# Routed experts' rows: places in one large table, or sums in two token tables

## The reference, cut to what matters

```python
def moe_ffn(x, router_w, router_bias, w1, w3, w2, sw1, sw3, sw2):
    ...
    _, idx = lax.top_k(scores + router_bias.astype(F32), TOP_K)      # TOP_K = 8 of 64
    gates = gates / jnp.sum(gates, -1, keepdims=True) * ROUTED_SCALE
    ...
        y = (jax.nn.silu(h @ w1[e]) * (h @ w3[e])) @ w2[e]           # h: the rows routed to e
        return y.astype(F32) * gate[:, None]
    ...
    routed = jnp.zeros((T, D), F32).at[row_tok].add(ys.reshape(n_rows, D))
    shared = (jax.nn.silu(xf @ sw1) * (xf @ sw3)) @ sw2
    return (routed + shared.astype(F32)).astype(x.dtype).reshape(B, S, D)
...
        x = layer_norm(DN_ALPHA * x + ffn, ln2_g[l], ln2_b[l])
```

## Time and profile before

| | |
|---|---|
| median of 3 runs | 2184.23 us (2182.27 to 2187.38) |
| profiled execution, its own time | 2186.5 us |
| its span, first to last instruction | 2184.7 us |
| PE busy | 2080.8 us, 95% |
| DVE busy | 1642.6 us, 75% |
| ACT busy | 1409.2 us, 65% |
| POOL busy | 581.3 us, 27% |
| moved by DMA | 572.78 MB |
| mean granted clock of PE | 0.978 |

### The profile page before, as it was taken

The page is one execution under the profiler, slowest core; times in us unless marked ns, Lnnn a source line. Parts: engine busy times, 40 slices in busy tenths (PEclk is TensorE's granted clock), DMA queues, the critical chain, the costliest instruction groups (busy, mean ns, idle before and its releaser), DMA issues. The chain is left out here.

```text
span 2184.7 us, 32260 instructions
## 1 busy us (share of the span) xinstructions
PE 2080.8 (95%) x10998; PEld 1689.3 (77%) x10998; DVE 1642.6 (75%) x2419; ACT 1409.2 (65%) x1778; POOL 581.3 (27%) x336
## 2 busy tenths in 40 slices
PE   6999989899999999999888999898999999999996
PEld 4778878688888888887376888777888888888862
DVE  2486453699999999998345944537999999999955
ACT  3443762488888888887045347426888888888841
POOL 0010200133443444442011021002344434434310
PEclk9999999999999999999999999999999999999998
DMA  6312213599999999995741140265999999999938
GB/s 202 97 30 72 113 67 147 196 378 377 389 378 379 375 387 386 382 382 223 302 145 59 51 162 1 76 252 192 382 378 393 378 375 382 376 382 380 379 128 359
DMA packets 136052, 572.78 MB, mean 262 GB/s; under 512 B 32356, under 2 KB 58468, under 8 KB 82712
## 3 DMA queue, kind: packets, MB, share of 16 engines
q1 hardware_dynamic: 99096, 504.37, 60.5%
q0 software_dynamic: 36864, 67.19, 8.0%
HBM read 560.41 MB, written 78.14 MB: 292 GB/s over the span
## 5 line engine op out<-in xcount | busy, mean ns | idle before, releaser
L1430 POOL DMA_INDIRECT rows<-x_rows,index x122 | 281.4, 2307 | 129.8 <-issue 69.5
L1587 DVE TENSOR_TENSOR w_next_lo<-w_next,w_hi 128x2048 fp32r<-128x2048 f32 x128 | 292.8, 2288 | 0.1
L1587 DVE TENSOR_TENSOR w_lo<-w,w_hi 128x2048 fp32r<-128x2048 f32 x124 | 285.2, 2300 | 2.0 <-ACT w_hi L1635 1.4
L1635 ACT CAST w_hi<-w 128x2048 fp32r<-128x2048 f32 x124 | 236.4, 1906 | 51.0 <-PE ps_sum L1493 51.0
L1635 ACT CAST w_hi<-w_next 128x2048 fp32r<-128x2048 f32 x128 | 243.5, 1902 | 35.4 <-PE ps_sum L1493 35.4
L1491 PE MATMUL ps_sum<-w_hi,rowsT_first_hi 128*128 128x512 f32 x512 | 208.8, 408 | 9.1 <-PEq L151 9.1
L1491 PE MATMUL ps_sum<-w_hi,rowsT_hi 128*128 128x512 f32 x512 | 208.0, 406 | 4.4 <-DVE rowsT_lo L1599 4.4
L1516 PE MATMUL ps_sum<-w_hi,hiddenT_hi 128*128 128x512 f32 x512 | 201.8, 394 | 3.9 <-DVE hiddenT_lo L1606 3.9
L1493 PE MATMUL ps_sum<-w_hi,rowsT_first_lo 128*128 128x512 f32 x512 | 202.9, 396 | 0.0
L1493 PE MATMUL ps_sum<-w_hi,rowsT_lo 128*128 128x512 f32 x512 | 202.3, 395 | 0.0
L1518 PE MATMUL ps_sum<-w_hi,hiddenT_lo 128*128 128x512 f32 x512 | 201.8, 394 | 0.0
(11 more groups left out here) (286 smaller groups left out, 5283.3 us busy)
## 6 DMA issues: line engine op xcount, KB each, us to landing
w_next<-exp_w SPq DMA_DIRECT2D x192, 1024.0 KB, 10.1
w<-exp_w SPq DMA_DIRECT2D x128, 1024.0 KB, 9.6
w_first<-exp_w SPq DMA_DIRECT2D x32, 1024.0 KB
w_last<-exp_w SPq DMA_DIRECT2D x32, 1024.0 KB
wbuf<-w_in SPq DMA_DIRECT2D x16, 1024.0 KB, 5.5
got<-y_rows SPq DMA_DIRECT2D x8, 2048.0 KB, 21.3
got<-y_rows SPq DMA_DIRECT2D x16, 1024.0 KB, 24.3
w_out_sb<-w_out SPq DMA_DIRECT2D x2, 4096.0 KB, 19.3
```

Of the source, the lines that this page charges most:

```text
L1430: pool.indirect_dma_start(rows[0:CAP, x.slot, :], None, d["x1_rows"], bass.IndirectOffsetOnAxis(ap=index[0:CAP, x.step, 0:1], axis=0), bou ...
L1587: dve.tensor_tensor(w13_lo[x.slot][:, :, k, :], w13[x.slot][:, :, k, :], w13_hi[:, :, k, :].bitcast(F32), ALU.subtract).then_inc(S["up_lo_ ...
L1635: act.copy(w13_hi[:, :, k, :], w13[x.slot][:, :, k, :]).then_inc(S["up_hi_b" if half else "up_hi_a"], 1)
```

## The change

The experts' rows are no longer kept apart until the end. There are two DRAM tables `sum_rows` of 512 x 1024, one row a token. A put is an indirect DMA with an addition: the row is added to the token's row in the table, expert by expert in the one and the other table in turn. It uses the token's number, so the place, its two columns and its second index fall away. Because two additions to the same row must not be under way together, `put` waits for the put two steps back, on the same table. SP clears both tables from a DRAM constant of zeros in the attention stage of each layer. In the second norm SP loads two rows a token in place of eight, PE adds both to `ps_sum`, and DVE takes scaled input plus `ps_sum` in one operation, with a tile's scaling moved behind the next tile's sum and centring. `r` has a buffer for each tile.

```diff
@@ -56,11 +56,10 @@
 MAX_PASSES = -(-SEQ // CAP)
 NOT_ROUTED = 1024.0
 ABSENT = 8192.0
-PLACES = SEQ * TOPK
-IDX, IDX_LOW, DEST, DEST_LOW, GATES = 0, 1, 2, 3, 4
-PART = 8
+IDX, IDX_LOW, GATES = 0, 1, 2
+PART = 6
+TABLES = 2
 TOKEN_AT = ROPE // 2
-PLACE_AT = TOKEN_AT + NT
 
 
 C_DQ, C_DK, C_DV = 0, 384, 768
...
@@ -114,6 +113,7 @@
         "c_once": once.astype(f),
         "c_row": row.astype(f),
         "c_mask": mask.astype(f),
+        "c_zero": np.zeros((SEQ, D), f),
         "c_onehot": onehot.astype(f),
         "c_addend": (addend / SCALE).astype(f),
     }
...
@@ -717,7 +717,10 @@
                 sp.dma_start(bias[:], d["bias_tiles"]).then_inc(S["bias_in"], 16)
                 sp.dma_start(sb["w_out"][:], d["w_out"][bass.ds(l, 1)].rearrange("o (p k) c -> p (o k) c", k=KD)
                              ).then_inc(S["w_out_in"], 16)
+                for j in range(TABLES):
+                    sp.dma_start(d["sum_rows"][j], d["c_zero"]).then_inc(S["sums_clear"], 16)
                 sp.wait_ge(S["w_out_in"], 16)
+                sp.wait_ge(S["sums_clear"], 16 * TABLES)
 
             @block.tensor
             def _(pe):
...
@@ -1073,11 +1076,11 @@
                 shared_up(3, 0, early, range(4, KD))
                 for q in (0, 2):
                     shared_up(q, early, SEQ).then_inc(S["up_made"], 1)
-                pe.wait_ge(S["tables"], 1)
-                pick(0, range(DEST, PART))
-                pick(1, range(DEST, PART))
+                pe.wait_ge(S["parts_cast"], 3)
+                pick(0, range(GATES, PART))
+                pick(1, range(GATES, PART))
                 shared_up(1, early, SEQ).then_inc(S["up_made"], 1)
-                pick(2, range(DEST, PART))
+                pick(2, range(GATES, PART))
                 shared_up(3, early, SEQ).then_inc(S["up_made"], 1)
                 pe.wait_ge(S["rows0_in"], 16)
                 pe.wait_ge(S["counted"], 1)
...
@@ -1127,8 +1130,6 @@
                 for q in range(3):
                     act.wait_ge(S["gate_left"], q + 1)
                     act.copy(parts[:, :, :, GATES + q], gate[:]).then_inc(S["parts_cast"], 1)
-                act.wait_ge(S["place_ready"], 1)
-                act.copy(parts[:, :, :, DEST], place[:]).then_inc(S["dest_cast"], 1)
                 for m in range(2):
                     act.wait_ge(S["up_made"], 2 * m + 1)
                     act.activation(act_out[:, m, :], up_bank[m], ACT.Silu).then_inc(S["silu_out"], 1)
...
@@ -1221,17 +1222,16 @@
                     reads += 1
                     return flat_x[0:CAP, ((reads - 1) % 2) * 512:((reads - 1) % 2) * 512 + n]
 
-                def whole(k, v, pair):
+                def whole(k, pair):
                     with nc.allow_low_precision(reason="sums of two whole numbers below 2**14"):
-                        return dve.tensor_reduce(index[0:CAP, k, v:v + 1], pair, AX.X, ALU.add).then_inc(S["index_ready"], 1)
+                        return dve.tensor_reduce(index[0:CAP, k:k + 1], pair, AX.X, ALU.add).then_inc(S["index_ready"], 1)
 
                 def tokens(k):
-                    whole(k, 0, picked(DEST))
+                    whole(k, picked(GATES))
 
                 def gates(k):
-                    got = picked(PART - DEST)
-                    dve.tensor_reduce(expert_gate[0:CAP, k:k + 1], got[:, GATES - DEST:GATES - DEST + 3], AX.X, ALU.add)
-                    whole(k, 1, got[:, 0:2])
+                    dve.tensor_reduce(expert_gate[0:CAP, k:k + 1], picked(PART - GATES)[:, 0:3], AX.X, ALU.add
+                                      ).then_inc(S["index_ready"], 1)
 
                 def less(q):
                     dve.wait_ge(S["parts_cast"], q + 1)
@@ -1253,13 +1253,7 @@
                 for k in range(FIRST):
                     tokens(k)
                 less(0)
-                for t in range(NT):
-                    o = dve.tensor_tensor_scan(place[:, t, :], mask[:, t, :], mask[:, t, :], 0.0, ALU.add, ALU.max)
-                step(o)
                 less(1)
-                for t in range(NT):
-                    o = dve.tensor_scalar(place[:, t, :], place[:, t, :], sb["row"][:, PLACE_AT + t:PLACE_AT + t + 1], None, ALU.add)
-                o.then_inc(S["place_ready"], 1)
                 step(dve.tensor_reduce(cnt[:, 0:1], ps_c[:, 0:NE], AX.X, ALU.max))
 
                 step(dve.tensor_scalar(cnt[:, 1:2], cnt[:, 0:1], float(CAP), 1.0, ALU.is_gt, ALU.add))
...
@@ -1268,9 +1262,6 @@
                                                   in1=cnt[:, q - 1:q], op0=ALU.is_gt, op1=ALU.add))
                 step(dve.tensor_scalar(cnt[:, 0:1], cnt[:, MAX_PASSES - 1:MAX_PASSES], float(NE // LAP), -float(NE // LAP), ALU.mult, ALU.add))
                 dve.tensor_copy(sb["laps_more"][:], cnt[:, 0:1]).then_inc(S["counted"], 1)
-                dve.wait_ge(S["dest_cast"], 1)
-                dve.wait_ge(S["parts_cast"], 3)
-                dve.tensor_tensor(parts[:, :, :, DEST_LOW], place[:], parts[:, :, :, DEST], ALU.subtract).then_inc(S["tables"], 1)
                 lower_up(0)
                 gates(0)
                 gates(1)
...
@@ -1428,16 +1419,18 @@
                         pool.wait_ge(S["rows_turned"], x.n - SLOTS)
                     pool.sem_inc(S["dma_turns"], 1)
                     pool.indirect_dma_start(rows[0:CAP, x.slot, :], None, d["x1_rows"],
-                                            bass.IndirectOffsetOnAxis(ap=index[0:CAP, x.step, 0:1], axis=0),
+                                            bass.IndirectOffsetOnAxis(ap=index[0:CAP, x.step:x.step + 1], axis=0),
                                             bounds_check=SEQ - 1, oob_is_err=False).then_inc(S[f"rows{x.slot}_in"], 16)
 
                 def put(x):
 
                     pool.wait_ge(S["y_made"], x.n + 1)
+                    if x.has(-TABLES):
+                        pool.wait_ge(S[f"y{x.slot % 2}_out"], 16 * (x.times(2) - 1))
                     pool.sem_inc(S["dma_turns"], 1)
-                    pool.indirect_dma_start(d["y_rows"], bass.IndirectOffsetOnAxis(ap=index[0:CAP, x.step, 1:2], axis=0),
-                                            y[x.slot % 2][0:CAP, :], None, bounds_check=PLACES - 1, oob_is_err=False
-                                            ).then_inc(S[f"y{x.slot % 2}_out"], 16)
+                    pool.indirect_dma_start(d["sum_rows"][x.slot % TABLES], bass.IndirectOffsetOnAxis(ap=index[0:CAP, x.step:x.step + 1], axis=0),
+                                            y[x.slot % 2][0:CAP, :], None, bounds_check=SEQ - 1, oob_is_err=False,
+                                            compute_op=ALU.add).then_inc(S[f"y{x.slot % 2}_out"], 16)
 
                 def step(x):
                     if x.has(-2):
@@ -1571,8 +1564,7 @@
                         dve.wait_ge(S[f"y{x.slot % 2}_out"], 16 * (x + -LAP).times(2))
                     dve.tensor_reduce(gate[0:CAP, x.step:x.step + 1], ps_p[0:CAP, GATES:GATES + 3], AX.X, ALU.add)
                     with nc.allow_low_precision(reason="sums of two whole numbers below 2**14"):
-                        dve.tensor_reduce(index[0:CAP, x.step, :], ps_p[0:CAP, 0:GATES].rearrange("p (v q) -> p v q", q=2),
-                                          AX.X, ALU.add).then_inc(S["index_ready"], 1)
+                        dve.tensor_reduce(index[0:CAP, x.step:x.step + 1], ps_p[0:CAP, 0:GATES], AX.X, ALU.add).then_inc(S["index_ready"], 1)
 
                 def hide(x):
                     b = x.slot % 2
...
@@ -1692,13 +1684,10 @@
 
 def _second_norm(nc, d, sb, l):
     with ExitStack() as ctx:
-        S = _named(ctx, nc, NORM_SEMS + " first_in " + " ".join(f"y{t}a_in y{t}b_in y{t}c_in" for t in range(NT))
-                   + " half_step half_summed summed x_ready")
-        QUARTER, HALF = TOPK // 4, TOPK // 2
+        S = _named(ctx, nc, NORM_SEMS + " first_in sum0_in sum1_in sum2_in sum3_in summed x_ready")
         T = lambda name, shape: ctx.enter_context(nc.sbuf_tensor(name, shape, F32))
-        got = T("got", [P, NT, TOPK, D])
-        half = T("half_sum", [P, 2, D])
-        r = T("r5", [P, 2, D])
+        got = T("got", [P, NT, TABLES, D])
+        r = T("r5", [P, NT, D])
         junk = T("junk5", [P, D])
         st = T("st5", [P, 5, NT])
         gain, shift = sb["rows"][:, 2, :], sb["rows"][:, 3, :]
@@ -1708,11 +1697,9 @@
         with nc.Block() as block:
             @block.sync
             def _(sp):
-                y = d["y_rows"].rearrange("(t p s) c -> t p s c", p=P, s=TOPK)
                 for t in range(NT):
-                    sp.dma_start(got[:, t, HALF:TOPK], y[t, :, HALF:TOPK]).then_inc(S[f"y{t}a_in"], 16)
-                    sp.dma_start(got[:, t, 0:QUARTER], y[t, :, 0:QUARTER]).then_inc(S[f"y{t}b_in"], 16)
-                    sp.dma_start(got[:, t, QUARTER:HALF], y[t, :, QUARTER:HALF]).then_inc(S[f"y{t}c_in"], 16)
+                    for j in range(TABLES):
```

(67 more changed lines are left out.)

## The result

The changed kernel takes 2130.57 us (median of 4 runs, 2129.5 to 2132.51) against 2184.44 for the kernel before on the same chip (median of 4): a ratio of 0.9754, 95% interval 0.9737 to 0.977. The profiled execution took 2129.5 us with a span of 2127.5; before, they were 2186.5 and 2184.7, so 57.2 us of span have to be accounted for.

What follows compares the result with a forecast made beforehand. TensorE bounds the expert loops, DMA close behind; DMA bounds the layer ends. 2186.5 - 44 - 1 + 2 = 2143.5, lowered to 2141 because the median lay 2.3 below the profiled run; range 2132 to 2190, or 2205 with rival 1's nearer part.

Steps and rivals of the forecast that it cites:

- Second norm: End stage of each layer: DVE's last step at 30.6 us instead of 52.7; gain 22 a layer, bounds 18 to 25.
- I enter 2 us in all: Expert loops of both layers: loss entered for the adding put, 2 us in all.
- PE's 9.65: Expert loops: TensorE's pace of 9.65 us an expert, against which the DMA demand was set.
- The adding put: Expert loops: each adding put costs the DMA engines 0.69 us more, making demand 9.73 us an expert.
- the lead: Expert loops: weight loads have 9.5 us of lead, more than the 5 us of excess demand, so loss 0.
- rival 1: Expert loops turn to the DMA's pace; an accumulated row costs three plain ones, 72 us lost, 2211 us; chance 0.22.
- Routing: Routing of each layer: fewer scans, additions and casts gain 0.5 us a layer, 1 in all, between 0 and 3.
- Clearing and the wait in `put`: Table clearing hides under busy PE, and POOL's wait for the put two back is already met: cost 0 each.
- Rival 5: Adding put and end-stage clock: the add costs nothing and the clock stays up, 2132 us; chance 0.08.

Runs made afterwards that it cites:

- e2: Changed kernel with `index` allocated at its old 64 bytes, so `region` lies 32 bytes lower, as in the kernel before: 2138.71 us, ratio 0.9785.
- e6c: Changed kernel with an extra load of 0.106 MB an expert that nobody reads: 2152.8 us.
- e11: Changed kernel with a plain put instead of the adding one and an unread extra load of 0.426 MB an expert: 2152.03 us.
- e4: Changed kernel with `parts` allocated 8 wide and used 6 wide, its stride and the addresses behind it as before, `region` staying: 2130.77 us.
- e3: Kernel before with a 32-byte spacer that moves `region` alone: 2178.03 us, ratio 0.9965.
- e9: Changed kernel with a 32-byte spacer ahead of `parts` and `index` at its old 64 bytes, both together: 2131.44 us.
- e10: Changed kernel with 32-byte spacers that shift only stationary operands (second `rowsT` pair, `hiddenT`), weights staying: 2144.0 us, ratio 0.9813.

## Why the prediction was wrong, point by point

- **Second norm: right.** In the last end stage the first tile is at PE after 5.1 us (forecast 5.7) and summed at 10.8 (11.4), the second 3.4 later (3.4), DVE's chain takes 19.0 us (19.2), its end is at 29.8 (30.6). Measured 23.7 and 22.9 a layer, entered 22, bounds 18 to 25.
- **The step that failed is "I enter 2 us in all" for the loop**, and behind it "PE's 9.65", which was taken as a constant of the kernel. The loop did go at PE's pace, but that pace was 9.59, and the two loops gave 7.5 us. e2 gives 7.4 of it back with 32 bytes of padding. The prediction listed the narrower `index` and `parts` as edits of the picks alone and did not ask what they move.
- **The adding put: right in price and demand** (0.70 and about 9.7 us), and the lead hides it. It was a nearer thing than I said: most of the lead was gone at the end of the first layer, and rival 1 would have begun with 0.1 MB more an expert, as e6c shows. The 0.70 is packet time; what a put costs where transfers set the pace was 0.56 (e11).
- **Routing: 4.0 us where 1 was entered**, above its bound of 3. Some 1.5 of it may be layout again (e2), and the wait for `tables` is 1.0. The stride of `parts` (e4) can't be told from the spread between traces, and some 1.5 us stay unassigned.
- **Clearing and the wait in `put`: right,** 0 and 0; the attention takes 90.96 us for 90.93.
- **The whole.** The spans shrank by 57.2 us where the terms made 43: 9.5 of the difference are the loop, 2.6 the end stages, 3.0 the routing, less 0.8 in all other stretches. The medians shrank by 53.9 only, because the profiled execution before was 2 us above its median and the one after 1 us below.
- With region at its old place the change gives 2138.7 (e2), 2.3 us from the forecast, and a part of that nearness is luck: beside e2 the kernel before took 2186.4, so the gain was 47.7 us where 43 were forecast.
- Rival 5 (2132) came near the time by another cause: the adding was not free, and the clock of the end stage was low after the change too (0.61 from 1047.2 to 1056 us, the wait and the first products).

## What to carry to other kernels

Before a change of a buffer's size is costed, list the addresses that it moves; a period that is PE's own can shift by a per cent through them (9.59 to 9.71 us here), and one padded run of each kernel separates that from the change. Look at the parts of such a run, though: e3 and e9 came out as expected in part through the clock of a few products. A resource can be asked for more than it has for as long as a lead lasts, so look at how landing times grow through the stage and not at whether anyone waits. If rows are added by DMA, use two tables: with one, the landing time of a put becomes the pace.

## What the runs showed of the hardware

- Down products of float32r (512 columns) stood 227 ns apart where moving less stationary address was a multiple of 128 bytes (changed kernel), and 233 ns where it left 96 (e10). For the products that read `w_next_lo` it was 227.6 ns at 0, 229.9 at 64 and 233 to 234 at 96.
- An indirect DMA of some 64 rows of 4 KB that adds into DRAM took 0.70 us more packet time on the 16 engines than one that writes, and 2.2 us of GpSimd's time instead of 1.7; where the loop goes at the transfers' pace it cost 0.56.
- After 2.02 us of waiting, PE's granted clock was 0.55 from 1028.2 to 1031.5 us in the changed kernel; in e9, after 1.99 us at the same place in the program, it stayed at 1.00.
